# Latent columns first in the input projection, and both attentions turned and scored two pairs of heads ahead

## What is computed

```
h    = rms_norm(x, g_norm1) * (1 + sc1) + sh1
proj = h @ w_in                     # 3904 columns: q_d 1024, k_d 1024, v_d 1024, cq 512, ckv 256, k_pe 64
q_d, k_d = rms_norm(...)            # 8 heads, two halves of 64 columns
a_out = differential_attention(q_d, k_d, v_d, lam, rel_bias)    # softmax(1) - lam * softmax(2)
q_m  = rms_norm(cq) @ w_q_b         # 8 heads of 192 columns (128 + 64 rotated)
kv   = rms_norm(ckv) @ w_kv_b       # 8 heads of 128 key + 128 value columns
b_out = latent_attention(rope(rms_norm(q_m)), rope(rms_norm(k_m)), v_m)
x    = x + gt1 * (concat[a_out, b_out] @ w_out)
```

## Time and profile before

| | us |
|---|---|
| median of 3 runs | 2366.39 (2362.44 to 2368.14) |
| the profiled execution | 2366.54 |
| its span, first to last instruction | 2364.8 |
| mean granted TensorE clock | 0.962 |
| PE, DVE, ACT, POOL busy | 2160.3, 1550.2, 997.2, 157.2 |

### The profile page before, as it was taken

One profiled execution on the slowest core, in us unless ns is written; L12 is line 12 of the kernel. 1 busy time (PEld: TensorE's weight loads), 2 busy tenths in 40 slices (PEclk: granted clock), 3 DMA queues, 4 the chain that ended last, 5 costly groups with the idle time before them and its releaser, 6 DMA issues.

```text
span 2364.8 us, 26656 instructions
## 1 busy us (share of the span) xinstructions
PE 2160.3 (91%) x9742; PEld 1747.9 (74%) x9742; DVE 1550.2 (66%) x1684; ACT 997.2 (42%) x1270; POOL 157.2 (7%) x213
## 2 busy tenths in 40 slices
PE   3789995567889999999999999999999999999997
PEld 2567884454767888888888888878687777888886
DVE  5875886663777775555455556478778788865554
ACT  5225444534335444433444454544343434444443
POOL 2000002110000000000000002530202000000000
PEclk9899997688989999999999999999999999999999
DMA  9996994041878886556766556655554555657553
GB/s 323 348 351 208 397 334 135 0 160 46 327 259 285 282 269 194 185 187 186 211 187 193 186 198 208 194 166 180 152 150 160 170 187 161 196 180 234 184 186 133
DMA packets 223262, 490.17 MB, mean 207 GB/s; under 512 B 15322, under 2 KB 17728, under 8 KB 221872
## 3 DMA queue, kind: packets, MB, share of 16 engines
q1 hardware_dynamic: 218080, 467.20, 60.6%
q0 software_dynamic: 4112, 17.16, 2.2%
q10 hardware_dynamic: 960, 4.35, 0.5%
HBM read 482.35 MB, written 6.29 MB: 207 GB/s over the span
## 4 chain that ended last, share of the span: by engine, by line
PE 78%; DVE 10%; DMA 6%; ACT 3%; issue 3%; ACTq 0%; POOL 0%; DVEq 0%; SPq 0%; POOLq 0%
PE psum L535 71%; DMA ring<-in_w_ada 3%; DVE w_lo L1623 2%; DVE acc L1643 2%; ACT w_hi L1069 1%; DVE acc_b L1643 1%; DMA raw<-in_w_gate 1%; PE psum L659 1%; DMA raw<-in_w_out 1%; PE psum L807 1%; PE psum L492 1%; PE psum L847 1%; PE psum L731 0%; DMA raw<-in_w_q_b 0%; PE psum L732 0%
## 5 line engine op out<-in xcount | busy, mean ns | idle before, releaser
L1623 DVE TENSOR_TENSOR w_lo<-raw,w_hi 128x1024 fp32r<-128x1024 f32 (+1 forms) x698 | 854.9, 1231 | 636.6 <-ACT w_hi L1069 616.0
L1069 ACT ACTIVATE w_hi<-raw 128x1024 fp32r<-128x1024 f32 (+1 forms) x698 | 735.4, 1056 | 1137.3 <-PE psum L535 897.3
L535 PE MATMUL psum<-w_hi,x_hi 128*128 128x512 f32 (+1 forms) x2048 | 815.6, 398 | 55.3 <-DVE w_lo L1623 55.2
L535 PE MATMUL psum<-w_hi,x_lo 128*128 128x512 f32 (+1 forms) x2048 | 801.1, 391 | 0.0
L535 PE MATMUL psum<-w_lo,x_hi 128*128 128x512 f32 (+1 forms) x2048 | 800.9, 391 | 0.0
L535 PEld LDWEIGHTS psum<-w_hi,x_hi 128*128 128x128 f32 x2048 | 388.6, 190 | 150.8 <-DVE w_lo L1623 41.8
L535 PEld LDWEIGHTS psum<-w_lo,x_hi 128*128 128x128 f32 x2048 | 388.2, 190 | 81.8
L535 PEld LDWEIGHTS psum<-w_hi,x_lo 128*128 128x128 f32 x2048 | 389.2, 190 | 78.1 <-issue 1.0
L535 PE MATMUL psum<-w_hi,f_hi 128*128 128x512 f32 x352 | 140.2, 398 | 0.0
L535 PE MATMUL psum<-w_lo,f_hi 128*128 128x512 f32 x352 | 139.5, 396 | 0.0
L535 PE MATMUL psum<-w_hi,f_lo 128*128 128x512 f32 x352 | 139.5, 396 | 0.0
(11 more groups left out here) (362 smaller groups left out, 1743.1 us busy)
## 6 DMA issues: line engine op xcount, KB each, us to landing
raw<-in_w_in SPq DMA_DIRECT2D x264, 512.0 KB, 4.2
ring<-in_w_ada SPq DMA_DIRECT2D x144, 512.0 KB, 6.5
raw<-in_w_gate SPq DMA_DIRECT2D x88, 512.0 KB, 3.7
raw<-in_w_up SPq DMA_DIRECT2D x88, 512.0 KB, 4.3
raw<-in_w_down SPq DMA_DIRECT2D x88, 512.0 KB, 3.6
raw<-in_w_out SPq DMA_DIRECT2D x64, 512.0 KB, 4.4
raw<-in_w_ada SPq DMA_DIRECT2D x48, 512.0 KB, 4.7
raw<-in_w_branch SPq DMA_DIRECT2D x48, 512.0 KB, 4.1
```

What stands on the lines that cost most here:

```text
L535: last = pe.matmul(pair(b)[:, a, 0:width], x[:, k, cut], w[:, s, kk, 0:width], start=(u == 0 and kk == 0 and n == 0), stop=(u == units - 1 ...
L1069: act.activation(w_hi[:, s, :, 0:width], raw[:, r, :, 0:width], ACT.Copy).then_inc(hi_ready, 1)
L1623: dve.tensor_tensor(w_lo[:, s, :, 0:width], raw[:, r, :, 0:width], w_hi[:, s, :, 0:width].bitcast(F32), ALU.subtract).then_inc(raw_used, 1)
```

## The change

The blocks of w_in are multiplied in the order 6, 7, 0 to 5. The latent columns are squared, scaled, turned and split during the third to fifth of them; the sums per head and the root of 64 columns come during the last. `bias_t` and `squares` now share memory, so the bias is loaded behind the sums per head. Of the eight folds `A8`, four (`A4`) stand one by one in the differential attention, four in the latent stage. In both attentions the operands are staged, turned and scored two pairs ahead; the loops are written out. The first units of w_q_b are multiplied before the last `turn_out` of the differential attention, the first four of w_out before the last one of the latent attention. The sums and the root of q and k are taken apart, q's within the latent products. VectorE waits for x in the second block of w_out.

```diff
+A4 = "aaaa"
+C_Q = ("gaagaa", "gaga", "gaga")
+IN_ORDER = (6, 7, 0, 1, 2, 3, 4, 5)
...
@@ TensorE
+            for n in range(1, 8):
+                begin(x_hi, x_lo, 0, 8, in_width(IN_ORDER[n]))
+                seg = B7 if n < 7 else B6
+                multiply(seg[:8])
+                if n == 4:
+                    turn_latent(4, 2)
+                multiply(seg[8:])
+                if n == 3:
+                    turn_latent(0, 4)
+                if n in (3, 5, 7):
                     sum_ada()
...
+            turn_diff(0)
+            pe.wait_ge(pair_taken[1], pl.n["block"] // 2 + 1)
+            score_diff(0)
+            turn_diff(2)
+            score_diff(2)
+            for i in range(HD // 2):
+                weigh_diff(i)
+                if i < HD // 2 - 2:
+                    turn_diff(4)
+                elif i == HD // 2 - 1:
+                    first_latent()
+                turn_out_diff()
+                if i < HD // 2 - 2:
+                    score_diff(4)
                 pl.step("head", 2)
...
+            def first_out():
+
+                pe.wait_ge(head_exp, pl.at("head", 2))
+                begin(x_hi, x_lo, 0, 8)
+                multiply(S0)
...
@@ ScalarE
+                if n == 2:
+                    evicted()
+                    square_latent()
+                if n == 4:
+                    high_latent(0)
+                    high_latent(2)
+                if n == 6:
+                    evicted()
+                    square_heads(0)
...
+            for i in range(HD // 2 - 1):
+                square_out()
                 weights_diff(2)
+                high_diff(i)
+                if i < HD // 2 - 2:
+                    begin_diff(4)
...
+            split(S0)
+            take_weights_mla()
+            high_mla(HD // 2 - 1)
...
@@ VectorE
+                if n == 3:
+                    scale_latent()
+                if n == 4:
+                    low_all(c_hi[:, 0:4, :], c_lo[:, 0:4, :], 4, True)
                 if n in (4, 6):
...
+                if n == 7:
+                    sum_heads(0)
+                    sum_heads(1)
+                work(seg[8:], width)
+                if n == 4:
+                    low_all(c_hi[:, 4:6, :], c_lo[:, 4:6, :], 2, True)
...
+            for i in range(HD // 2 - 1):
+                if i < HD // 2 - 2:
+                    for s in range(2):
+                        stage_diff(i, s, 2)
+                scores_diff(i, 2)
                 scale_diff()
+                work("a")
+                mix_diff(2)
                 end_diff(i)
...
+            work("gg")
             scale_mla()
+            work("gg")
             end_mla(HD // 2 - 1)
...
-            dve.wait_ge(x1_in, 16)
             for b in range(4):
...
+                if b == 1:
+                    dve.wait_ge(x1_in, 16)
...
@@ GpSimd
+            pool.wait_ge(norm_asked, pl.at("norm", 1))
+            for a in range(TT):
+                pool.dma_start(bias_t[:, :, a, :],
...
-            inverse_root(None, 32, 192)
+            inverse_root(None, 16, 192)
+            inverse_root(None, 16, 192, 16)
```

More of the change, by code:

```diff
@@ L243, in build @@
             lg = sb("lg", [P, 2, 2, W], stack=ph)
+            c_hi = sb("c_hi", [P, 6, SEQ], F32R, stack=ph)
+            k_pe = sb("k_pe", [P, TT, 64], stack=ph)
+            pe_gain = sb("pe_gain", [P, 2, 64], stack=ph)
+            rtmp = sb("rtmp", [P, TT, HD, 32], stack=ph)
+            q_pe = sb("q_pe", [P, TT, HD, 64], stack=ph)
+            sb("beside_folds", [P, 640], stack=ph)
+            c_lo = sb("c_lo", [P, 6, SEQ], F32R, stack=ph)
+            with ExitStack() as q:
+                squares = sb("squares", [P, 2, D], stack=q)
             bias_t = sb("bias_t", [P, HD, TT, SEQ], stack=ph)
@@ L675, in begin_diff, with score_diff @@
                     last.then_inc(head_turned, 1)
+            def score_diff(ahead):
                 for s in range(2):
                     pe.wait_ge(head_taken, pl.at("head", ahead + s + 1))
-                    if s == 1 and not ahead:
+                    if ahead:
+                        pe.wait_ge(head_max, pl.at("head", ahead + s - 1))
+                    elif s == 1:
                         pe.wait_ge(ada_taken, pl.at("ada", 1))
@@ L691, in end_diff, with turn_out_diff, first_latent @@
                 for s in range(2):
-                    weigh(s, stT[:, s, 1, :], lambda kt: proj[:, kt, bass.ds(i * 256 + (2048 + s * P), P)], pl.at("head", s + 1))
-                then()
+                    weigh(s, stT[:, s, 1, :], lambda kt: proj[:, kt, i * 256 + 2048 + s * P:i * 256 + 2048 + (s + 1) * P],
+                          pl.at("head", s + 1), 4 * s + 3)
+            def turn_out_diff():
                 for s in range(2):
-                    turn_out(s, staged[:, s, 4:6, :], pl.at("head", s + 1))
-                pl.step("head", 2)
[L698 to L706, removed]
+                    turn_out(s, staged[:, s, 4:6, :], pl.at("head", s + 1), 4 * s + 3)
+            def first_latent():
+                begin(c_hi, c_lo, 0, 2)
+                multiply(C_Q[0])
+            multiply(A4)
+            pe.wait_ge(pair_taken[0], (pl.n["block"] + 1) // 2 + 1)
+            pe.wait_ge(chunks_taken, pl.at("chunk", 2))
+            turn_diff(0)
[12 more added lines that the diff above has]
+                    score_diff(4)
+                pl.step("head", 2)
+            pe.wait_ge(head_done, pl.at("head", 0))
+            for b in range(1, 3):
                 begin(c_hi, c_lo, 0, 2)
-                multiply("gaga" if b < 2 else "gg")
+                multiply(C_Q[b])
             for b in range(4):
@@ L1261, in _ @@
             copy_out(proj[:, :, 2 * W:3 * W], 1)
+            evicted()
+            for a in range(TT):
+                act.activation(squares[:, a, 0:1536], qm[:, a, :], ACT.Square).then_inc(latent_squared, 1)
+            pl.step("norm")
             for b in range(1, 4):
@@ L1870, in _ @@
             pl.step("head", 2)
-            for b in range(3):
-                work("gaga" if b < 2 else "gg")
-            for b in range(4):
-                work("ga")
-            pl.step("block", 7)
-            take_ada(7)
+            work(C_Q[1] + C_Q[2] + "ga")
             dve.wait_ge(pe_in, 32)
```

316 lines of the change are left out of this document (168 added, 148 removed).

## The result

The changed kernel takes 2356.34 us (median of 5 runs, 2355.51 to 2359.88) against 2366.51 of the kernel before (5 runs, 2362.44 to 2369.27): a ratio of 0.995 with a 95% interval of 0.9933 to 0.9966. It is faster, by 10 us where 26 were forecast; 2356 lies above the range of 2331 to 2352.

A forecast was written before the change was run, and what follows sets the result against it. TensorE was busy 91% of the span, with room only between 371.1 and 594.6. A gain of 31.3 us before the latent attention less 5.5 given back gave -25.8 from 2366.54: 2340.7, say 2341; range 2331 to 2352.

The forecast's parts named there:

- w_in, 372.9 forecast: End of the w_in stage: 371.1 plus 1.8 us for moved latent turns and the narrow block gives 372.9.
- The power: GpSimd's scale and power of 64 columns in the head norms, forecast ready 0.1 us before the last w_in product.
- The lock between GpSimd and VectorE: Rival 3's first cause: GpSimd's power holds back w_lo in w_in's last block, 11.8 us; rival's total 2350, chance 0.10.
- First weights at 387.4: Differential attention: turns of the first weights start at 387.4 instead of 408.71, 21.3 us gained.
- three periods of 42.1: Differential attention: periods of 12.9, 14.2 and 15.0 us, 42.1 together against 51.5, 9.4 us gained.
- rival 4: Differential attention: pairs scored ahead only stand before the weights, period stays 17.07; 9.4 us less gain, 2350, chance 0.08.
- The first latent turns at 493.4: After the latent stage, the latent attention's first turned operands come at 493.4 instead of 524.69, 31.3 us gained.
- The latent attention, 72.3 us to head_done: Latent attention from its start to head_done: 22.5 + 26.6 + 9.5 + 12.2 + 1.5 = 72.3 us instead of 58.3.
- The eighth w_lo 24.5 us after head_done: w_out start: loads and x, 8.4 MB at 0.4 MB/us, plus latency, a split and w_lo: 24.5 us, before 30.9.
- The credit of 6.4 us: Start of w_out: 6.4 us saved after head_done, with four units done and no wait for x.
- 5.5 taken out of 7.6: Latent attention's net loss: 14.0 - 6.4 = 7.6 us at most, taken as 5.5 expecting some products under the copies.
- The chance of 0.17: Rival 2: latent attention loses nothing, its period drops to 12.03 us of TensorE work, products hide in waits; 2333, chance 0.17.

The follow-up runs named there:

- e12: The changed kernel itself, unaltered, measured once more: 2354.54 us, ratio 0.9944.
- e10: e1 with the differential attention also put back to one pair ahead: 2346.66 us, ratio 0.9909.
- e3: Changed kernel plus 12 useless TensorE transposes ahead of the later pairs' scores in the latent attention: 2350.51 us, ratio 0.9919.
- e4: Changed kernel with ScalarE copying the next operands before the ending pair's high parts in the latent attention: 2346.98 us, ratio 0.9909.
- e11: Changed kernel, latent operands copied before high parts, four w_out units behind last turn_out, 22 useless transposes before the second latent pair's scores: 2325.78 us.
- e1: Changed kernel with latent attention one pair ahead again and the first four w_out units behind the last turn_out: 2334.79 us, ratio 0.9852.
- e2: Changed kernel with only the latent attention's look-ahead put back to one pair: 2349.83 us, ratio 0.9915.
- e5: Changed kernel with only the first four w_out units put behind the last turn_out: 2343.75 us, ratio 0.9897.
- e9: e1 with VectorE's wait for x put ahead of its first w_lo of w_out: 2339.52 us, ratio 0.9879.

## Why the prediction was right and wrong

- **w_in, 372.9 forecast.** 372.8 in e12. Right: no wait of TensorE, the reductions under the last block, bias never waited for. The power was forecast to end 0.1 us before the last product and ended 1.5 after it; it took 11.45 us itself, not the 10.55 of the earlier trace rows.
- **The lock between GpSimd and VectorE** did not hold: two w_lo took 2.48 us, 1.24 each, within a power of 11.46; before it was the same. The Trainium skill ("SBUF — State Buffer", "SBUF: two separate sides") has a VectorE operation with two SBUF inputs contend with one of GpSimd that reads SBUF; the trace of the changed kernel disagrees as that of before did.
- **First weights at 387.4, three periods of 42.1.** 387.76 and 41.6 in e12. Right as sums, but by luck: the errors of the parts (4.0, 0.7 and -4.7 us) cancel. ScalarE's operands come late for the scores in the first two periods (3.51 us), while the third has nothing ahead of it and is 10.3. That rival 4, pairs that only stand in front, is wrong here was shown by e10.
- **The first latent turns at 493.4.** 494.09 in e12, 0.7 late. The differential attention ended at 444.9 (445.7 forecast), the stage behind it took 49.2 us (47.7, though its terms add up to 47.5). Here too errors cancel in part: the wait for the last product was 5.02 us where 2.5 were counted.
- **The latent attention, 72.3 us to head_done.** It took 81.4: this is the step that failed, in the sentence that its chain "stays 13 to 14 us against 14.20". The list of that chain was complete, but ScalarE's order in it (weights, high parts, then operands) leaves TensorE without work for 1.71 us just before its longest row of products, and the durations were taken at the clock of the earlier trace rows. Measured, the period is 16.2 to 16.3 us. The first pair's weighted sums ended 26.2 us after the start (22.5 forecast), the two periods between weighted sums took 33.3 (26.6), the last 9.3 (9.5), the four units and the end 12.6 (13.7): 3.7 + 6.7 - 0.2 - 1.1 = 9.1. e3, e4 and e11 show the cause.
- **The eighth w_lo 24.5 us after head_done**, 26.6 in e12: a term too small by 2.1. The 0.4 MB/us in it rests on no row that is shown; the changed kernel moved 368 GB/s on average over that stretch, 9.7 MB where 8.4 were counted. The credit of 6.4 us was for the early units and the late wait for x together; by e1, e2 and e5 the units bring 0.5 to 2.1 us of it, and the rest of the 4.3 us gained on the 30.9 of the earlier trace rows belongs to the late wait (e9).
- **5.5 taken out of 7.6**, in the hope of products under the copies: they did not come, 2.1 us.
- **The rest.** Of the 11.8 us that e12's eighth w_lo is earlier than before, 9.9 are left in the span: 1.9 given back behind it, of which no run shows the place.

The sum for e12, whose profiled execution took 2356.59 us: 0.7 + 9.1 + 2.1 + 2.1 + 1.9 = 15.9 us over the 2340.7 forecast. What was priced rightly is the time of the four units in front of the last turn_out, 10.9 to 12.2 us forecast and 11.2 measured; what was wrong was the credit set against it, and to see the units as part of a change that had to be taken whole. The chance of 0.17 went to the opposite error, that the period would drop to TensorE's own work. With one swap on ScalarE it does, and lower than thought, to 10.7 us.

## What to carry to other kernels

Before deepening a look-ahead, write down for each engine in which order it serves the old pair and the new one: whatever the next long row of products waits for goes first, or the look-ahead opens the gap that it was to close. Work moved ahead of a release is free only if nothing that the release starts is the bound behind it; where loads are, release first and compute under them. Price TensorE's stages with the clock that the new gaps will leave, not with that of the old period.

## What the runs showed of the hardware

A wait of 1.71 us inside the busy latent attention was followed by a fall to the low level, 1.2 GHz, that came only in the work behind it and lasted 10.2 us. Windows of e12, first in the wait, then behind it:

```profile
522.50:524.20 1.70, 0.00 (x1) 0.00 (x0) 1.40 (x5) 1.70 (x6) 0.00 (x0) 1.00 0.00 0
524.20:525.90 1.70, 1.69 (x6) 0.89 (x6) 1.50 (x7) 1.16 (x3) 0.00 (x0) 0.97 0.00 0
525.90:536.10 10.20, 10.20 (x30) 6.28 (x29) 1.82 (x5) 2.61 (x9) 0.00 (x0) 0.50 0.01 2
```

The clock is full in the wait and falls 1.7 us into the work behind it, where TensorE is busy all the time; so the row that shows the low clock is not the row that caused it. Waits of 0.32 to 0.53 us in the same place (e11, e3, e1) had no such effect. The Trainium skill ("TensorE: Matmul & The Clock Gate", "A second HAM failure mode: psum-queue depth-cycling") tells of short idle times between groups of matmuls that make the clock swing between its two levels; the trace agrees, 1.00 and 0.50 within one period.

The kernel before has such a wait too, of 1.54 us, ahead of the turns of the weights instead of the scores. Windows of it and of what follows:

```profile
547.77:549.31 1.54, 0.00 (x1) 0.01 (x1) 1.08 (x5) 1.54 (x7) 0.00 (x0) 1.00 0.00 0
549.75:553.15 3.40, 3.30 (x16) 2.94 (x15) 2.24 (x9) 1.60 (x4) 0.00 (x0) 0.51 0.00 0
```

There the low level lasts only 3.4 us, in each period, and in e1 as well. So the look-ahead did not bring the fall; it moved the wait, and the low stretch behind it became three times as long. Why the one lasts 3.4 us and the other 10.2 stays open.

Filling such a wait with 12 to 22 useless transposes of 0.12 us each made the attention shorter: 73.6 us against 81.4 (e3), 49.6 against 54.0 (e11).
